# Spreading a 4 KB row with TensorE instead of by DMA, and cutting one output tile in two to fill the end of an attention

## What is computed

```python
cs = jax.nn.silu(c)                       # c: one row of 1024 numbers
mod = cs @ w_ada[l] + b_ada[l]            # 6 x 1024 modulation values
shift1, scale1, gate1, shift2, scale2, gate2 = ...split(mod, 6)
h = rms_norm(x, norm1_g[l]) * (1 + scale1) + shift1
proj = h @ w_in[l]                        # lora, recurrence, gates of the merge
attn = mla_attention(...)                 # 8 heads
rec = rg_lru_branch(...)                  # gated linear recurrence
y = g_attn * (attn @ w_o_attn[l]) + g_rec * (rec @ w_o_lru[l])
x = x + gate1 * (y @ w_out[l])
h2 = rms_norm(x, norm2_g[l]) * (1 + scale2) + shift2
x = x + gate2 * peer_ffn(h2, ...)         # 16 of 16384 experts per head and token, gathered rows
```

## Time and profile before

| | us |
|---|---|
| median of 3 runs (lowest, highest) | 1594.84 (1592.02, 1595.03) |
| profiled execution, device time | 1594.12 |
| its span, first to last instruction | 1592.1 |
| PE busy | 1449.5 (91%) |
| DVE busy | 863.4 (54%) |
| ACT busy | 483.9 (30%) |
| POOL busy | 298.2 (19%) |

### The profile page before, as it was taken

The page is one execution under the profiler, slowest core; times in us unless marked ns, Lnnn a source line. Parts: engine busy times, 40 slices in busy tenths (PEclk is TensorE's granted clock), DMA queues, the critical chain, the costliest instruction groups (busy, mean ns, idle before and its releaser), DMA issues.

```text
span 1592.1 us, 25602 instructions
## 1 busy us (share of the span) xinstructions
PE 1449.5 (91%) x10126; PEld 1179.1 (74%) x10126; DVE 863.4 (54%) x2304; ACT 483.9 (30%) x1269; POOL 298.2 (19%) x277
## 2 busy tenths in 40 slices
PE   9999999998979888989888899999999999988887
PEld 7888999997978788878887757888755555444444
DVE  6678777868686868686865536612352222212212
ACT  2364224544444444444443412210111111111111
POOL 0000003454444444443444100000000000000000
PEclk9999999998999999999999999999799999999999
DMA  9947969999999999999999966575589999999997
GB/s 370 413 189 289 365 224 381 417 421 420 421 419 420 414 410 422 421 420 417 421 421 420 398 270 277 212 308 220 212 370 432 431 426 432 431 429 431 433 429 318
DMA packets 62740, 595.95 MB, mean 374 GB/s; under 512 B 7088, under 2 KB 8624, under 8 KB 15152
## 3 DMA queue, kind: packets, MB, share of 16 engines
q1 hardware_dynamic: 23328, 317.21, 48.2%
q0 software_dynamic: 39312, 277.37, 42.2%
HBM read 593.50 MB, written 1.05 MB: 373 GB/s over the span
## 4 chain that ended last, share of the span: by engine, by line
PE 57%; DMA 25%; DVE 12%; ACT 3%; issue 2%; POOL 0%; SPq 0%; DVEq 0%; POOLq 0%; ACTq 0%
PE bank L1057 14%; DMA weight_slabs<-in_w_moe 11%; DMA weight_slabs<-in_expert_uv,work 10%; PE bank L748 10%; PE bank L1239 5%; PE bank L1212 4%; PE bank L950 3%; PE bank L1111 3%; DVE weight_slabs L2133 2%; PE bank L1267 2%; PE bank L774 2%; PE bank L871 2%; DMA gathered_rows<-in_expert_uv,work 2%; DVE gathered_rows L2133 1%; PE bank L979 1%
## 5 line engine op out<-in xcount | busy, mean ns | idle before, releaser
L1057 PE MATMUL bank<-work,gathered_rows 128*128 128x128 f32 x2048 | 263.5, 287 | 45.9 <-ACT work L1539 45.9
L1057 PEld LDWEIGHTS bank<-work,gathered_rows 128*128 128x128 f32 x2048 | 256.5, 203 | 55.2 <-ACT work L1539 51.1
L1057 PE MATMUL bank<-work,weight_slabs 128*128 128x128 f32 x2048 | 256.8, 283 | 35.8 <-ACT work L1539 35.7
L1057 PEld LDWEIGHTS bank<-work,weight_slabs 128*128 128x128 f32 x2048 | 248.4, 198 | 44.3 <-ACT work L1539 42.4
L2133 DVE CUSTOM_DVE_ANT_0 weight_slabs<-weight_slabs,work 128x1024 f32<-128x1024 f32 x128 | 155.4, 1223 | 84.3 <-DMA weight_slabs<-in_expert_uv,work 84.0
L2133 DVE CUSTOM_DVE_ANT_0 gathered_rows<-gathered_rows,work 128x1024 f32<-128x1024 f32 x128 | 155.2, 1223 | 76.4 <-DMA gathered_rows<-in_expert_uv,work 75.2
L748 PE MATMUL bank<-hT,weight_slabs 128*128 128x256 f32 x832 | 184.6, 382 | 0.0
L1631 POOL DMA_INDIRECT gathered_rows<-in_expert_uv,work x128 | 139.8, 1092 | 213.1 <-PE bank L1057 176.5
L1631 POOL DMA_INDIRECT weight_slabs<-in_expert_uv,work x128 | 149.0, 1164 | 163.4 <-PE bank L1057 159.5
L748 PEld LDWEIGHTS bank<-hT,weight_slabs 128*128 128x128 f32 x832 | 158.1, 191 | 24.8 <-issue 3.6
L2376 DVE COPY work<-bank 128x512 f32<-128x512 f32 x32 | 22.1, 690 | 245.4 <-PE bank L1200 245.4
(11 more groups left out here) (397 smaller groups left out, 1822.0 us busy)
## 6 DMA issues: line engine op xcount, KB each, us to landing
weight_slabs<-in_slabs SPq DMA_DIRECT2D x44, 2048.0 KB, 10.4
weight_slabs<-in_w_moe SPq DMA_DIRECT2D x20, 4096.0 KB, 29.2
weight_slabs<-in_w_moe SPq DMA_DIRECT2D x25, 2048.0 KB, 25.4
gathered_rows<-in_w_moe SPq DMA_DIRECT2D x9, 4096.0 KB, 34.2
dots_ring<-in_w_moe SPq DMA_DIRECT2D x10, 2048.0 KB, 31.8
weight_slabs<-in_slabs SPq DMA_DIRECT2D x16, 512.0 KB, 12.5
dots_ring<-in_slabs POOLq DMA_DIRECT2D x16, 512.0 KB, 8.7
gathered_rows<-in_slabs SPq DMA_DIRECT2D x8, 512.0 KB, 13.2
```

Of the source, the lines that this page charges most:

```text
L1057: ins = nc.tensor.matmul(ps[2 * t + c // 4][:, (c % 4) * P:(c % 4 + 1) * P], row_at[k][:, D + c * P:D + (c + 1) * P], diag[:, k, :], start ...
```

## The change

The row c is loaded once, to one partition, and PE copies it to all 128 by two matmuls with a one-row matrix of ones, into two banks that are not yet in use ("lg0" and "lx3", 512 numbers each). ACT takes Silu from the banks, in two instructions, and PE opens the bank of "lx3" only after that. The matrix of ones is written by DVE, and the identity matrix is loaded after the third weight chunk. At the end of the first attention half of "yla3" moves behind `weighted(1)`, one quarter of "ylb0" moves between `turn_heads(1)` and `attended`, and the later quarters each move one place up; the wait for "aAT1" moves behind the moved quarter. In the plan "yla3" now stands after "aO1", so the two change banks.

```diff
@@ first_fill
     for i in range(4):
-        fill[4 + i] = [(f"yla{i}", "D", [])]
+        fill[4 + i if i < 3 else HEADS] = [(f"yla{i}", "D", [])]
@@ SP
-        sp.dma_start(crow[:, :], g["c_row"].partition_broadcast(P)).then_inc(c_in, 16)
+        sp.dma_start(crow[0:1, :], g["c_row"].partition_broadcast(1)).then_inc(c_in, 16)
         for half in range(2):
             sp.dma_start(xT[:, 4 * half:4 * half + 4, :], ...).then_inc(x_in[half], 16)
-        sp.dma_start(cst[:, 0:2 * P], g["constants"][:, 0:2 * P]).then_inc(consts_in, 16)
         sp.dma_start(cols[:, :], g["columns"]).then_inc(cols_in, 16)
...
             if c == 2:
+                sp.dma_start(cst[:, 0:P], g["constants"][:, 0:P]).then_inc(extras_in, 16)
@@ PE, attention
             fill(HEADS + 1)
-            wait_emptied(pe, f"{tag}AT1")
+            if tag == "b":
+                wait_emptied(pe, "bAT1")
@@ PE, opening (C_BANKS = ("lg0", "lx3"))
+        pe.wait_ge(ones_ready, 1)
+        pe.wait_ge(c_in, 16)
+        for half, name in enumerate(C_BANKS):
+            nc.tensor.matmul(bank(name)[:, :], ones[0:1, :], crow[0:1, half * 512:(half + 1) * 512], start=True, stop=True).then_inc(c_spread, 1)
         pe.wait_ge(zero_ready, 2)
         for name in STREAMED:
+            if name in C_BANKS:
+                pe.wait_ge(silu_ready, 1)
             nc.tensor.matmul(begin(name)[:, :], zero, opening, start=True, stop=False)
         b = begin("ss1")
-        pe.wait_ge(consts_in, 16)
@@ PE, fill of the first attention
                 i = h - 4
-                ...            (32 passes of yla{i})
+                first_lru(i, 0, 2 if i < 3 else 1)
+            elif h == HEADS:
+                first_lru(3, 1, 2)
@@ PE, after the first attention
-        attended("a", 0)
         begin("ylb0")
         recurrent("ylb0", 0, 1)
+        wait_emptied(pe, "aAT1")
+        attended("a", 0)
+        recurrent("ylb0", 1, 2)
         pe.wait_ge(y_ready, 1)
...
-        recurrent("ylb0", 1, 2)
+        recurrent("ylb0", 2, 3)
         sum_tile(0)
-        done(recurrent("ylb0", 2, 4))
+        done(recurrent("ylb0", 3, 4))
@@ ACT
-        act.wait_ge(c_in, 16)
-        A(crow[:, :], crow[:, :], ACT.Silu).then_inc(silu_ready, 1)
+        act.wait_ge(c_spread, 2)
+        A(crow[:, 0:512], bank(C_BANKS[0])[:, :], ACT.Silu)
+        A(crow[:, 512:D], bank(C_BANKS[1])[:, :], ACT.Silu).then_inc(silu_ready, 1)
@@ DVE
+        V.memset(ones, 1.0).then_inc(ones_ready, 1)
         V.memset(work[:, 6168:6168 + 512], 0.0).then_inc(zero_ready, 1)
...
-        dve.wait_ge(extras_in, 64)
+        dve.wait_ge(extras_in, 80)
...
             heads_out(tag, nth, 1)
+            fill(HEADS)
...
-            if h >= 4:
-                i = h - 4
+            if h >= 4 and h != HEADS - 1:
+                i = min(h - 4, 3)
                 freed(f"yla{i}", ...)
```

More of the change, by code:

```diff
@@ L343, in wait_emptied @@
         eng.wait_ge(emptied[e], evacs(e, n))
+    C_BANKS = ("lg0", "lx3")
     VARS = {n: i + 1 for i, n in enumerate(("lora", "aqk", "bqk"))}
@@ L433, in program @@
     x_in = [sem(f"x_half{i}_in") for i in range(2)]
-    consts_in, cols_in, extras_in = sem("consts_in"), sem("columns_in"), sem("extras_in")
+    cols_in, extras_in = sem("columns_in"), sem("extras_in")
     c_in, c2_in, dots_done = sem("c_row_in"), sem("c_row_2_in"), sem("slab_dots_done")
@@ L439, in program @@
     act_step = sem("act_step")
-    zero_ready = sem("zero_ready")
+    zero_ready, ones_ready, c_spread = sem("zero_ready"), sem("ones_ready"), sem("c_row_on_all_partitions")
     silu_ready, square_ready = sem("silu_ready"), sem("square_ready")
@@ L917, in beside, with first_lru @@
                 i = h - 4
[L918 to L923, removed]
+                first_lru(i, 0, 2 if i < 3 else 1)
+            elif h == HEADS:
+                first_lru(3, 1, 2)
+        def first_lru(i, q0, q1):
+            b = begin(f"yla{i}") if q0 == 0 else bank(f"yla{i}")
+            w = slab3(8, 512)(slab(f"o_lru{i // 2}"))
+            for q in range(q0, q1):
+                for k in range(DC):
+                    f0 = (2 * (i % 2) + q) * P
+                    last = nc.tensor.matmul(b[:, q * P:(q + 1) * P], w[:, k, f0:f0 + P], gate4[:, 0, k, :], start=(k == 0), stop=(k == DC - 1))
+            if q1 == 2:
                 done(last)
@@ L1960, in beside @@
                 slab_dots(f"ada{5 + h}")
-            else:
+            elif h < HEADS:
                 slab_dots(f"ada{9 + (h - 4) // 2}", 2 * (h % 2), 2 * (h % 2) + 2)
```

## The result

The changed kernel takes **1594.89 us** (median of 15 runs, 1593.06 to 1598.38), the kernel before, run beside it, 1592.95 (15 runs, 1591.94 to 1595.03). The ratio is 1.0015, with a 95% interval of 1.0008 to 1.0022: about 2 us slower. The interval lies clear of 1, so the change does cost time, but less than the 0.2% that I called no change. The profiled execution took 1596.72 us with a span of 1594.6, against 1594.12 and 1592.1 before.

What follows compares the result with a forecast made beforehand. PE was taken to bound the opening, and the PE, ACT and DVE chain everything before the first gather. A gain of 2.4 less a loss of 2.4 summed to 0.0: median 1594.9 us, 8-in-10 range 1592.0 to 1598.0.

Steps and rivals of the forecast that it cites:

- rival D: Opening: the constants were the bound, so it gains 1.2 us instead of losing 2.4, giving 1591.3 us; chance 6%.
- c lands at 2.7: Opening: the 4 KB load of c, issued at 0.73, takes 2.0 us and lands at 2.7 (bounds 2.4 and 5.4).
- Rival C: Opening: c lands as late as the broadcast did, 4.7 us after its issue, giving 1597.6 us; chance 8%.
- Four slow passes, twelve zero passes at 0.43: Opening on PE after c lands: four slow passes take 3.53 us, then twelve quick zero passes take 5.16.
- Rival A: Opening: the quick pace comes later, each slow pass costing 0.4 us more, giving 1596.6 to 1600 us; chance 10%.
- The opening loses 2.4: Opening: the sum of squares ends at 15.3 instead of 12.90, a loss of 2.4 us (2.1 to 5.1).
- The fill holds the clock: First attention's end: with PE's gaps filled the granted clock stays up, saving the 1.66 us its fall cost.
- rival B: First attention's end: the fill does not hold the clock, so the low bound holds, 1596 us; chance 15%.
- DVE is late next, by the weight load: Before the output projection: DVE's dot products wait for a load landing at 196.20, leaving PE idle 0.45 us.
- 0.4 before the first query: Second norm: PE newly waits about 0.4 us for the first normed piece before the first query.
- The end gains 2.4: First attention's end: 3.26 us of gaps and clock less 0.45 and 0.4 of new waits (bounds 1.35 and 2.9).
- A shift of the first gather is a shift of the end: From first gather to kernel's end: moving the first gather, issued at 239.77 us, moves the end one to one.

Runs made afterwards that it cites:

- e6: Kernel before with the changed attention end, and DVE's dot products on the late weight load moved behind both combining steps, some ring dots later too: 1590.99 us, ratio 0.9990.
- e7: Kernel before with only the matrix of ones written by DVE and the identity loaded after the third weight chunk; c stays a broadcast: 1592.86 us, ratio 1.0004.
- e2: Changed kernel with the end of the first attention taken back, so the changed opening alone: 1598.31 us, ratio to before 1.0031.
- e5: The changed kernel again, with no edit: 1594.13 us, ratio to before 1.0008.
- e4: Kernel before with its zero passes cut to one row of zeros, nothing else moved: 1597.92 us, ratio 1.0030.
- e3: Changed kernel with c's wait and its two matmuls moved behind the first two 128-row zero matmuls: 1595.98 us, ratio to before 1.0021.
- e1: Kernel before with only the end of the first attention changed: 1591.42 us, ratio to before 0.9992.
- e8: The same kernel as e3, run once more for a second profile: 1596.81 us.

## Why the prediction was right, and where not

The forecast of no change holds, and the median meets the number almost exactly (1594.9 against 1594.89). That exactness is partly luck: the kernel before, run beside it, took 1592.95 and not the 1594.84 shown, so the change is +1.9 us where my sum was 0.0, and the forecast number met the median only because the median it started from lay 1.9 too high. By the sign that I had set, wrong if the first chunk starts after 21, the account of the opening is wrong (21.52), though the time came out. Step by step:

- **PE is the bound of the opening, not the constants**: right in the traces of before and after; in e6 the constants come last, by 0.39 us. e7 takes them away and gains nothing that can be measured; rival D, at its price, is refuted. DVE's wait for its weight chunk and Silu cost nothing either, as counted.
- **c lands at 2.7**: it landed earlier. It took 1.38 us from the issue (1.45 in e2, 1.51 in e5) and the first pass started at 2.24. Rival C is refuted.
- **A one-row pass costs what a slow 128-row pass does**: right (3.75 for four, against 3.53).
- **"Four slow passes, twelve zero passes at 0.43"**: the step that failed. The zero passes took 7.36 instead of 5.16. The sum lets the four one-row passes for c stand for the four slow passes of before; they replaced no slow pass, and five more slow ones followed. The count of four was itself that of one execution: the opening of before has four to eight. Rival A, which I gave 10%, is what happened, near the low end of its price of 1.7 to 5 us; e4 shows its mechanism by itself. "PE is as busy as before" was the wrong argument against it.
- **The opening loses 2.4**: it lost 4.3 in the profile: against the sum, -0.46 for c, +0.22 for its passes and +2.20 for the zero passes. Over the profiles it lost 3.9.
- **The fill holds the clock**: right, in six profiles; rival B did not come about in any. The 1.66 us for it is there only in executions in which the old end falls, three of four.
- **DVE is late next, by the weight load**: right in kind. Counted from the first chunk, the load landed 0.63 us later than before (201.15 - 21.52 against 196.20 - 17.20), so DVE waited 1.72 and PE 1.07 instead of 0.45; over the profiles with the new end and the old order of DVE, PE's wait ran from none (e3) to 1.59 (e1). My step took the landing from a row that varies: DVE's wait for that load is 0.75 to 2.65 in the nine profiles with the order of before.
- **0.4 before the first query**: 0.58.
- **The end gains 2.4**: 1.7 in the profile, 2.0 over the profiles.
- **A shift of the first gather is a shift of the end**: the pair agrees (2.74 and 2.5). But from the first gather to the end the ten profiles take 1347.9 to 1353.3, a spread larger than the effect, so a single pair could not have shown it.

The terms that were mis-sized thus add up: +1.9 in the opening and +0.7 at the end make +2.6 on the sum of 0.0, and the profiled execution is 1596.72 - 1594.12 = 2.6 slower. That the two agree to the tenth is luck as well, by the spread just named.

## What to carry to other kernels

Where PE starts slow, as here, passes on one row cost the slow price and leave the slow stretch still to come; count them as added to it. Four passes on all 128 rows ahead of them were not enough to be sure of the quick pace (e3 and e8). Before a DMA is taken off a queue, see whether the engine that waits for it was free at that moment: the wait for the constants ended when PE did, and taking it away was worth nothing that the times show. After gaps are filled, look for the load that is late next: here it decided from one execution to the next whether the gain reached the following stage, until the work that waits for it was moved behind. Then the next late load took 1.0 us back, so follow the gain to the end of the chain before counting it.

## What the hardware showed that I had not expected

**The quick pace of the opening comes at different times.** With 128-row passes from 1.58 on, they turned quick at 5.1 (before), 4.8 (e6), 7.5 (e7) and 8.2 us (e1), after four to eight slow passes; what sets the moment is open. The row of the granted clock does not tell it. In the window from 2 to 4 us of the kernel before it reads 1.00, which would be the higher of the two levels, while three passes are counted in 2 us, which at 0.43 each hold more than four:

```profile
2.00:4.00 2.00, 2.00 (x3) 0.76 (x3) 0.00 (x0) 0.01 (x1) 0.00 (x0) 1.00 1.05 293
```

So in these traces the pace of the opening must be read from the spacing of the weight loads.

**A load of 4 KB at the head of the queue takes 1.38 to 1.51 us from issue to landing** (after, e2, e5). The Trainium skill (DMA: Bandwidth & Descriptors, "Anatomy of one DMA") gives about 2.0 us of fixed time, for DMAs that GpSimd issues. This one is issued by SP, so the trace does not test that figure, and the row decides.

**A weight load is as long for one row as for 128**, 0.33 against 0.34 us at the slow pace. The Trainium skill (TensorE: Matmul & The Clock Gate, "LDWEIGHTS") says so, and the trace agrees; what the one-row pass does not share is the effect on the pace.
